# Stick-breaking mixer: the product of each unit's first head moves from VectorE to GpSimd

## The chip, the cores and the metric

The kernel runs on one core of a Trainium2 chip. The metric is the device time of one launch in microseconds (us). Three runs of the kernel before took 3267.1, 3270.11 and 3271.65 us; the median is 3270.11 us. Engines are called by the names of the profile: PE (TensorE), DVE (VectorE), ACT (ScalarE), POOL (GpSimd), SP (SyncE).

## The reference

One inference step of a two-layer encoder, for a prompt of 1024 rows and a sample of 64 rows that has 256 cached rows. The change lies in one of four mixers, the stick-breaking attention with 8 heads of width 64:

```
def sb_core(k, v, k_pos, q, q_pos):
    z = einsum('bqhd,bshd->bhqs', q, k) * HEAD_DIM ** -0.5
    mask = k_pos < q_pos
    log_beta = log_sigmoid(z)
    log_1m = where(mask, log_sigmoid(-z), 0.0)
    after = cumsum(log_1m, axis=3, reverse=True) - log_1m
    a = where(mask, exp(log_beta + after), 0.0)
    return einsum('bhqs,bshd->bqhd', a, v)
```

So a weight is sigmoid(z) of its key, times the product of sigmoid(-z) over all later keys that are still before the query. All is float32.

## The kernel before

The kernel is a row of phases (projections, attentions, feed-forward), and each phase is a block of one instruction stream per engine. The first instruction of a phase stands behind the end of the phase before on all engines. The attention phases come from one function, `attention(kind)`; the change touches kind "d", the stick-breaking one, called `stick` in the code; its tiles are named att_d_... in the trace.

The work of this phase is cut into 36 units: 4 pairs of heads, and in each pair 9 query tiles (`ALL`). Tile t (0 to 7) has 128 queries and 128(t+1) keys, so 128 to 1024 columns; the ninth tile is the sample, 64 queries and 320 keys. A unit holds both heads of its pair. For each unit:

- PE makes the scores of both heads in PSUM (L1059, with the mask added at L1070).
- ACT makes sigmoid(-z) into `rest` (L1196) and sigmoid(z) into `prob` (L1201), for each head.
- DVE runs along the keys backwards with a running product, `rest` into `left` (`scan`, L1285), and multiplies `prob` by `left` shifted by one column, in place (`weigh`, L1295). `remain(i)` puts both scans of a unit first, then both products. So DVE issues: scan head 0, scan head 1, product head 0, product head 1.
- PE transposes `prob` into PSUM (L1098), ACT copies that to SBUF (L1152), PE multiplies it with the values (L1127), and DVE copies the result out of PSUM (`output`, L1301). There is one PSUM bank for these results, so the product of a unit waits for the copy of the unit before it.

The order on each engine is written out by hand. DVE does `output(i - 2)` and then `remain(i + 2)`. PE transposes unit i, makes the scores of unit i + 3, and multiplies unit i - 1 with its values. There are four `prob` buffers per head, two of `rest` and two of `left`. A scan into `left` waits until the product that read the same buffer, two units back, is done (the semaphore `prob_ready` of its head); the transposes of PE wait for the same semaphore. A product waits for its own scan (`scan_done`) and for ACT's sigmoids (`taken_done`).

GpSimd sets one column of each `left` buffer to 1 in this phase (L1026) and has nothing else to do. In the three other attention phases it scales `prob` by a number per row (L1034, one tensor input), between DVE's reciprocal and PE's transposes.

DVE also has a scan with two SBUF inputs in the phase of kind "b", in which GpSimd scales: `select` (L1363 to L1370), five DVE instructions for each of six tiles, late in that phase.

Of the kernel before, what the change touches and what calls it, by code (L numbers as in the profile page):

```python
# [9 lines left out]
ALU = mybir.AluOpType  # L10
# [8 lines left out]
SEQ, DEC, PAST = 1024, 64, 256  # L19
# [18 lines left out]
FROM = 1  # L38


class Phase:
# [12 lines left out]
    def sb(self, name, shape, dt=F32):  # L54
        return self.ctx.enter_context(self.nc.sbuf_tensor(f"{self.name}_{name}", shape, dt))
# [7 lines left out]
    def sem(self, name):  # L63
        s = self.ctx.enter_context(self.nc.semaphore(f"{self.name}_{name}"))
        self.sems.append(s)
        return s
# [43 lines left out]
def key_tile(t):  # L110

    return (P * (t + 1), 0) if t < NT else (PAST + DEC, SEQ)
# [698 lines left out]
def queries(t):  # L811
    return DEC if t == NT else P
# [9 lines left out]
ALL = [(p, t) for p in range(PAIRS) for t in range(TILES)]  # L822
# [9 lines left out]
def chunks(i):  # L832

    w = key_tile(ALL[i][1])[0]
    return [(0, 0, 512), (1, 512, w - 512)] if w > 512 else [(i % 2, 0, w)]


def chunks_until(i):
    return sum(len(chunks(j)) for j in range(i + 1))
# [50 lines left out]
def attention(nc, dram, consts, kind, src, home, fetch=None):  # L890
# [15 lines left out]
    with Phase(nc, f"att_{kind}") as ph:  # L906
# [17 lines left out]
        ring = ahead + 1  # L924
        prob = [[sb(f"prob{s}{h}", [P, SEQ]) for h in range(2)] for s in range(ring)]
        if mla or fox:
            hidden = sb("hidden", [P, SEQ], BF16)
        if stick:
            rest = [[sb(f"rest{s}{h}", [P, SEQ]) for h in range(2)] for s in range(2)]
            left = [[sb(f"left{s}{h}", [P, SEQ + 1]) for h in range(2)] for s in range(2)]  # L930
# [5 lines left out]
        cleared, staged = sem("cleared"), sem("staged")  # L936
# [3 lines left out]
        prob_ready = [sem(f"prob_ready{h}") for h in range(2)]  # L940
# [7 lines left out]
        if stick:  # L948
            rest_done = [sem(f"rest_done{h}") for h in range(2)]
            taken_done = [sem(f"taken_done{h}") for h in range(2)]  # L950
            scan_done = [sem(f"scan_done{h}") for h in range(2)]
# [39 lines left out]
        @block.sync  # L991
        def _(eng):
            def load_w(p):
                eng.dma_start(wkv[p % 2][:], dram["w_b_ukv"][0, :, p * 2 * P:(p + 1) * 2 * P]).then_inc(w_in[p % 2], 16)

            def load_q(p):
                eng.dma_start(q[p % 2][:], dram["qbT"][2 * p:2 * p + 2].rearrange("h d t -> d h t")).then_inc(q_in[p % 2], 16)

            if fetch is not None:
                if fetch.x is not None:  # L1000
                    eng.dma_start(fetch.x[:], dram["x1"][0:P]).then_inc(fetch.x_in, 16)
                fetch.fetch_soon(eng)
            if mla:
                for p in range(2):
                    load_w(p)
                    load_q(p)
            for i, (p, t) in enumerate(ALL):
                if mla and t == 0 and 0 < p < PAIRS - 1:
                    eng.wait_ge(tp_ready, FROM + groups.jobs[p, 8] + 1)
                    load_w(p + 1)  # L1010
                    for h in range(2):
                        eng.wait_ge(s_ready[h], FROM + i)
                    load_q(p + 1)

        @block.gpsimd
        def _(pool):
            g = nc.gpsimd
            if mla or fox:
                g.memset(hidden[:, 0:SEQ - P], 0.0).then_inc(cleared, 1)
                g.tensor_copy(hidden[:, SEQ - P:], mask[:]).then_inc(cleared, 1)  # L1020
            if fox:
                g.memset(src["qT"][:, :, TOK:], 0.0).then_inc(staged, 1)
            if stick:
                for s in range(2):
                    for h in range(2):
                        g.memset(left[s][h][:, SEQ:SEQ + 1], 1.0).then_inc(cleared, 1)  # L1026
                return
            for i, (p, t) in enumerate(ALL):
                n, w = queries(t), key_tile(t)[0]
                for h in range(2):  # L1030
                    pr = prob[i % ring][h][0:n, 0:w]
                    c = 2 * (i % ring) + h
                    pool.wait_ge(rcp_done[h], FROM + i + 1)
                    g.tensor_scalar(pr, pr, rr[0:n, c:c + 1], 1.0, ALU.mult, ALU.mult).then_inc(prob_ready[h], 1)  # L1034
# [219 lines left out]
        def _(dve):  # L1254
# [23 lines left out]
            def scan(i, h):  # L1278
                p, t = ALL[i]
                n, w = queries(t), key_tile(t)[0]  # L1280
                dve.wait_ge(rest_done[h], FROM + chunks_until(i))
                if i >= 2:
                    dve.wait_ge(prob_ready[h], FROM + i - 1)
                r = rest[i % 2][h][0:n, 0:w][:, ::-1]
                v_.tensor_tensor_scan(left[i % 2][h][0:n, SEQ - w:SEQ][:, ::-1], r, r, 1.0, ALU.mult, ALU.bypass).then_inc(scan_done[h], 1)  # L1285

            def weigh(i, h):
                p, t = ALL[i]
                n, w = queries(t), key_tile(t)[0]
                if i == 0:  # L1290
                    dve.wait_ge(cleared, FROM + 4)
                dve.wait_ge(scan_done[h], FROM + i + 1)
                dve.wait_ge(taken_done[h], FROM + chunks_until(i))
                pr = prob[i % ring][h][0:n, 0:w]
                v_.tensor_tensor(pr, pr, left[i % 2][h][0:n, SEQ - w + 1:SEQ + 1], ALU.mult).then_inc(prob_ready[h], 1)  # L1295

            def output(i):
                p, t = ALL[i]
                n = queries(t)
                dve.wait_ge(pv_done, FROM + i + 1)  # L1300
                v_.tensor_copy(home[:, p, t * P:t * P + n], O[:, 0:n]).then_inc(o_out, 1)  # L1301
# [70 lines left out]
            if stick:  # L1372
                def remain(i):
                    for h in range(2):
                        scan(i, h)
                    for h in range(2):
                        weigh(i, h)

                for i in range(ahead - 1):
                    remain(i)  # L1380
                for i in range(n_units):
                    if i >= 2:
                        output(i - 2)
                    if i + ahead - 1 < n_units:
                        remain(i + ahead - 1)
                for i in (n_units - 2, n_units - 1):
                    output(i)
                return
# [964 lines left out]
```

## Time and profile before

| | |
|---|---|
| median of three runs | 3270.11 us |
| the profiled execution's own time | 3271.4 us |
| its span | 3269.6 us |
| PE busy | 2994.6 us (92%) |
| DVE busy | 1742.8 us (53%) |
| ACT busy | 1280.6 us (39%) |
| POOL busy | 169.4 us (5%) |
| mean granted TensorE clock | 0.955 |

All times in the rows are from one profiled execution. A row of the timeline may merge several like instructions that follow each other (x2). DVE instructions are stamped so that the next often starts 0.08 us before the one in front of it ends. The stick-breaking phase runs from about 2176 to 2341 us of the span.

### The profile page before, as it was taken

What the parts mean: (1) busy time and instruction counts of PE and PEld (TensorE: products, weight loads), DVE (VectorE), ACT (ScalarE), POOL (GpSimd) and SP (SyncE); (2) the same over time, 40 slices, a digit from 0 to 9 for tenths busy, and PEclk for the clock granted to TensorE, in tenths of its full rate; (3) what the DMA queues carried; (4) which work ended last, traced back from release to release, by engine and by line L of the source; (5) the groups of instructions that cost most, each with busy time, mean ns of one, the idle gap of its engine ahead of it and who ended that gap; (6) DMA issues with size and microseconds to landing.
All of it is one profiled execution on the core that took longest, in us unless ns stands there. A gap on an engine that the chain in (4) does not pass through costs nothing. (4 is left out here: it accounts for less than half of the span.)

```text
span 3269.6 us, 48973 instructions
## 1 busy us (share of the span) xinstructions
PE 2994.6 (92%) x17421; PEld 2533.1 (77%) x17421; DVE 1742.8 (53%) x3767; ACT 1280.6 (39%) x2682; POOL 169.4 (5%) x240
## 2 busy tenths in 40 slices
PE   6984887799899999999989798988898999999998
PEld 5771445468899999999989566865688999999998
DVE  4438788765455444444441465148754444444545
ACT  4334787463322222222243355357533222222223
POOL 0000222330000000000000131000000000000000
PEclk9995999899999999999989799999999999999999
DMA  4110100101211111111221201120201111111112
GB/s 133 51 33 3 37 13 1 46 30 47 69 51 38 51 38 38 51 38 51 79 96 55 85 2 49 52 71 1 76 0 52 51 38 39 51 38 51 38 38 75
DMA packets 147231, 152.09 MB, mean 47 GB/s; under 512 B 18156, under 2 KB 123236, under 8 KB 147108
## 3 DMA queue, kind: packets, MB, share of 16 engines
q1 hardware_dynamic: 147108, 150.54, 15.0%
q8 instruction: 66, 1.08, 0.1%
q14 instruction: 57, 0.47, 0.0%
HBM read 126.75 MB, written 23.24 MB: 46 GB/s over the span
## 5 line engine op out<-in xcount | busy, mean ns | idle before, releaser
L223 PE MATMUL ffn_up<-hlow_r,ffn_uhi 128*128 128x384 f32 (+1 forms) x2112 | 691.5, 327 | 0.0
L2107 DVE SCALAR_TENSOR_TENSOR ffn_cv<-ffn_G,ffn_ctap,ffn_cv 128x256 f32<-128x256 f32 (+1 forms) x352 | 168.9, 501 | 493.0 <-ACT ffn_cv L2033 488.3
L223 PEld LDWEIGHTS ffn_up<-hlow_r,ffn_uhi 128*128 128x128 f32 x2112 | 398.3, 189 | 0.9
L2027 ACT ACTIVATE ffn_G<-ffn_up 128x384 f32<-128x384 f32 (+2 forms) x176 | 65.3, 398 | 824.0 <-PE ffn_up L224 824.0
L2140 DVE TENSOR_TENSOR xres<-ffn_dn,xres 128x512 f32<-128x512 f32 (+1 forms) x396 | 263.6, 687 | 132.5 <-PE ffn_dn L224 121.2
L222 PE MATMUL ffn_dn<-ffn_dhi,ffn_ahi 128*128 128x512 f32 x704 | 280.7, 399 | 2.9
L224 PE MATMUL ffn_dn<-ffn_dhi,ffn_alo 128*128 128x512 f32 x704 | 278.3, 395 | 0.0
L223 PE MATMUL ffn_dn<-ffn_dlo_r,ffn_ahi 128*128 128x512 f32 x704 | 278.3, 395 | 0.0
L222 PE MATMUL ffn_up<-mixed_c_r,ffn_uhi 128*128 128x384 f32 (+1 forms) x528 | 174.6, 331 | 5.9 <-DVE ulo_r L2084 5.9
L222 PE MATMUL ffn_up<-mixed_a_r,ffn_uhi 128*128 128x384 f32 (+1 forms) x528 | 174.6, 331 | 5.7 <-DVE ulo_r L2084 5.7
L222 PE MATMUL ffn_up<-mixed_b_r,ffn_uhi 128*128 128x384 f32 (+1 forms) x528 | 174.2, 330 | 0.0
L222 PE MATMUL ffn_up<-mixed_d_r,ffn_uhi 128*128 128x384 f32 (+1 forms) x528 | 174.0, 330 | 0.0
L222 PEld LDWEIGHTS ffn_dn<-ffn_dhi,ffn_ahi 128*128 128x128 f32 x704 | 132.2, 188 | 42.4 <-DVE xres L2140 12.5
L224 PEld LDWEIGHTS ffn_dn<-ffn_dhi,ffn_alo 128*128 128x128 f32 x704 | 132.2, 188 | 32.0
L223 PEld LDWEIGHTS ffn_dn<-ffn_dlo_r,ffn_ahi 128*128 128x128 f32 x704 | 132.3, 188 | 29.9
L2038 ACT ACTIVATE ffn_cv<-ffn_cv 128x384 f32<-128x384 f32 x132 | 67.0, 508 | 182.4 <-DVE ffn_cv L2107 182.4
L222 PE MATMUL out_mm<-out_whi,out_ahi 128*128 128x512 f32 x256 | 104.0, 406 | 9.1 <-DVE wo_even_r L1803 4.6
L2119 DVE TENSOR_TENSOR ffn_alo<-ffn_cv,ffn_ahi 128x384 fp32r<-128x384 f32 x132 | 68.0, 515 | 77.5 <-ACT ffn_ahi L2042 77.5
L2114 DVE TENSOR_TENSOR ffn_cv<-ffn_up,ffn_cv 128x384 f32<-128x384 f32 x132 | 70.8, 536 | 69.1 <-ACT ffn_cv L2038 69.1
L2033 ACT ACTIVATE ffn_cv<-ffn_G,ffn_ctap 128x384 f32<-128x384 f32 (+2 forms) x176 | 103.6, 612 | 4.4
L222 PEld LDWEIGHTS ffn_up<-mixed_c_r,ffn_uhi 128*128 128x128 f32 x528 | 99.6, 189 | 6.7 <-DVE ulo_r L2084 6.3
L222 PEld LDWEIGHTS ffn_up<-mixed_a_r,ffn_uhi 128*128 128x128 f32 x528 | 99.6, 189 | 6.6 <-DVE ulo_r L2084 6.1
(474 smaller groups left out, 6965.9 us busy)
## 6 DMA issues: line engine op xcount, KB each, us to landing
ulo<-in_w_up_dram SPq DMA_DIRECT2D x44, 512.0 KB, 5.0
ffn_ulo<-in_w_up_dram SPq DMA_DIRECT2D x44, 512.0 KB, 4.7
ffn_dlo<-in_w_down_dram SPq DMA_DIRECT2D x22, 1024.0 KB, 4.9
w_d<-in_w_in_odd_dram SPq DMA_DIRECT2D x7, 768.0 KB, 9.9
proj_even_x<-in_x_prompt_dram SPq DMA_DIRECT2D x8, 512.0 KB, 3.4
xres<-in_x_prompt_dram SPq DMA_DIRECT2D x8, 512.0 KB, 4.5
scratch_x<-xres SPq DMA_DIRECT2D x8, 512.0 KB, 3.5
x_d<-scratch_x SPq DMA_DIRECT2D x8, 512.0 KB, 3.9
```

Of the source, the lines that this page charges most:

```text
L222: nc.tensor.matmul(out, lh, rh, start=first, stop=False)
L223: nc.tensor.matmul(out, lh, rl, start=False, stop=False)
L224: return nc.tensor.matmul(out, ll, rh, start=False, stop=last)
L2027: s.activation(G[:, g0:g0 + w], upbank(c, b, 0)[:, j:j + w], ACT.Copy).then_inc(g_out, 1)
L2033: last = s.activation(cv[:, 0, j:j + w], G[:, g0 - 2:g0 - 2 + w], ACT.Identity, scale=ctap[:, c, 0:1], bias=ctap[:, c, 3:4])
L2038: s.activation(cv[:, 1, 0:n], cv[:, 0, 0:n], ACT.Silu).then_inc(silu_done, 1)
L2107: last = v.scalar_tensor_tensor(cv[:, 0, j:j + w], G[:, g0 - 2 + tapno:g0 - 2 + tapno + w], ctap[:, c, tapno:tapno + 1], cv[:, 0, j:j + w] ...
L2114: v.tensor_tensor(cv[:, 1, 0:n0], upbank(c, b, 1)[:, 0:n0], cv[:, 1, 0:n0], ALU.mult).then_inc(a_done, 1)
L2119: last = v.tensor_tensor(to, cv[:, 1, c0 - t0:c1 - t0], ahi[:, c, c0:c1].bitcast(F32), ALU.subtract)
L2140: v.tensor_tensor(xs, dn[j % 4][0:n, :], xs, ALU.add).then_inc(half_added if t == NT else dn_added, 1)
```

## The change

GpSimd makes the product of head 0 of every unit; DVE keeps both scans and the product of head 1. The waits, the buffers and the semaphores that are raised are the same; the product of head 0 now raises `prob_ready[0]` from GpSimd.

```
             if stick:
                 ... memset of the column of ones
+                pool.wait_ge(cleared, FROM + 4)
+                for i, (p, t) in enumerate(ALL):
+                    n, w = queries(t), key_tile(t)[0]
+                    pool.wait_ge(scan_done[0], FROM + i + 1)
+                    pool.wait_ge(taken_done[0], FROM + chunks_until(i))
+                    pr = prob[i % ring][0][0:n, 0:w]
+                    g.tensor_tensor(pr, pr, left[i % 2][0][0:n, SEQ - w + 1:SEQ + 1], ALU.mult).then_inc(prob_ready[0], 1)
                 return
...
                 def remain(i):
                     for h in range(2):
                         scan(i, h)
-                    for h in range(2):
-                        weigh(i, h)
+                    weigh(i, 1)
```

## Rows read from the trace of the kernel before

**Rows 1.** Windows: busy us and instruction count of each engine in stretches of the phase
```profile
core 0: us, PE busy (x) PEld busy (x) DVE busy (x) ACT busy (x) POOL busy (x), PEclk, DMA share, GB/s
2177.00:2341.00 164.00, 138.69 (x1213) 91.18 (x1212) 140.05 (x180) 122.98 (x322) 0.00 (x0) 0.95 0.06 24
2218.03:2257.23 39.20, 32.54 (x309) 21.53 (x307) 34.90 (x46) 30.52 (x80) 0.00 (x0) 1.00 0.01 2
2221.35:2250.87 29.52, 23.00 (x186) 13.95 (x184) 29.03 (x31) 24.95 (x64) 0.00 (x0) 1.00 0.00 1
```
**Rows 2.** Waits around the phase: who for whom, us in total, times, longest
```profile
DVE mixed_d L1301 <- PE att_d_o L1127: 21.7, 11, 4.2
PE att_d_o L1127 <- DVE mixed_d L1301: 14.6, 9, 3.7
ACT L1196 <- PEq L74: 3.2, 1, 3.2
ACT out_ahi L1770 <- PEq L74: 3.0, 1, 3.0
```
**Rows 3.** Timeline of DVE alone, from the widest unit to the next pair
```profile
2244.04 4.47 DVE L1285 TENSOR_TENSOR_SCAN att_d_left<-att_d_rest 128x1024 f32<-128x1024 f32 x2
2248.42 2.34 DVE L1295 TENSOR_TENSOR att_d_prob<-att_d_prob,att_d_left 128x1024 f32<-128x1024 f32 x2
2250.67 0.29 DVE L1301 COPY mixed_d<-att_d_o 128x128 f32<-128x128 f32 x1
2250.87 1.52 DVE L1285 TENSOR_TENSOR_SCAN att_d_left<-att_d_rest 64x320 f32<-64x320 f32 x2
2252.32 0.86 DVE L1295 TENSOR_TENSOR att_d_prob<-att_d_prob,att_d_left 64x320 f32<-64x320 f32 x2
2253.31 0.72 DVE L1285 TENSOR_TENSOR_SCAN att_d_left<-att_d_rest 128x128 f32<-128x128 f32 x2
2253.95 0.46 DVE L1295 TENSOR_TENSOR att_d_prob<-att_d_prob,att_d_left 128x128 f32<-128x128 f32 x2
2257.02 0.29 DVE L1301 COPY mixed_d<-att_d_o 128x128 f32<-128x128 f32 x1 [2.61 <-PE att_d_o L1127]
2258.41 0.73 DVE L1295 TENSOR_TENSOR att_d_prob<-att_d_prob,att_d_left 128x256 f32<-128x256 f32 x2
2260.34 0.29 DVE L1301 COPY mixed_d<-att_d_o 128x128 f32<-128x128 f32 x1 [1.20 <-PE att_d_o L1127]
```
**Rows 4.** Windows of L1295 alone: the products of one pair's six wide units
```profile
2221.00:2251.00 30.00, 10.02 (x12) 1.00 0.00 1
```
**Rows 5.** Groups by form: one-input GpSimd instructions: busy us, mean ns, idle before
```profile
L1034 POOL TENSOR_SCALAR att_a_prob<-att_a_prob,att_a_rr 128x1024 f32<-128x1024 f32 x8 | 9.0, 1124 | 12.7 <-DVE att_a_rr L1276 12.7
L1034 POOL TENSOR_SCALAR att_a_prob<-att_a_prob,att_a_rr 128x384 f32<-128x384 f32 x8 | 4.7, 588 | 6.1 <-DVE att_a_rr L1276 6.1
L1034 POOL TENSOR_SCALAR att_a_prob<-att_a_prob,att_a_rr 64x320 f32<-64x320 f32 x8 | 4.2, 528 | 9.7 <-DVE att_a_rr L1276 9.2
L1020 POOL COPY att_b_hidden<-mask_chunk 128x128 bf16<-128x128 bf16 x1 | 0.9, 915 | 0.0
L1020 POOL COPY att_c_hidden<-mask_causal 128x128 bf16<-128x128 bf16 x1 | 0.3, 293 | 0.0
```
**Rows 6.** Timelines of GpSimd and of DVE around 565 us, in phase "b"
```profile
565.20 1.41 POOL L1034 TENSOR_SCALAR att_b_prob<-att_b_prob,att_b_rr 64x320 f32<-64x320 f32 x1 [0.23 <-DVE att_b_rr L1276]
...
565.03 0.66 DVE L1363 TENSOR_SCALAR att_b_tie<-scores,top_bits 128x896 bf16<-128x896 f32 x1
565.61 0.67 DVE L1364 TENSOR_SCALAR att_b_below<-scores,top_bits 128x896 bf16<-128x896 f32 x1
566.21 2.27 DVE L1366 TENSOR_TENSOR_SCAN att_b_beyond<-att_b_tie,att_b_spare 128x896 bf16<-128x896 bf16 x1
568.51 1.09 DVE L1368 SCALAR_TENSOR_TENSOR att_b_beyond<-att_b_beyond,att_b_tie 128x896 bf16<-128x896 bf16 x1
```
**Rows 7.** Groups by form: the same scan at the two neighbouring widths
```profile
L1366 DVE TENSOR_TENSOR_SCAN att_b_beyond<-att_b_tie,att_b_spare 128x1024 bf16<-128x1024 bf16 x1 | 2.3, 2347 | 0.0
L1366 DVE TENSOR_TENSOR_SCAN att_b_beyond<-att_b_tie,att_b_spare 128x768 bf16<-128x768 bf16 x1 | 1.8, 1805 | 0.0
```

## The prediction

> **What bounds the kernel now.** Over the whole span PE is the busy engine, but the change lies in one phase, so I read that phase alone. First the waits at its two ends: ACT's first instruction waits for the release of the phase before, and so does its first in the phase behind [rows 2]. What this phase loses or gains therefore goes into the span in full, with nothing else beside it to hide it. Then the windows: in the phase's 164.00 us DVE is busy for 140.05, PE for 138.69, ACT for 122.98 and GpSimd for nothing [rows 1]. These shares are too near each other to name the bound, so the next window holds one period of a pair of heads (39.20 us, DVE 34.90) and the last one only its six wide units, 384 to 1024 columns: 29.03 of 29.52 us on DVE, against 24.95 on ACT and 23.00 on PE. There DVE is the bound without a gap. The rest of the period is the turn from pair to pair (the units of 320, 128 and 256 columns). There DVE waits for PE before its copies, 2.61 and 1.20 us in this pair [rows 3], 21.7 us in the phase, at most 4.2 us at once [rows 2]. PE in turn waits 14.6 us for those copies [rows 2], because there is one bank for its results and each copy stands in DVE's queue behind a whole unit of scans and products. So the time of a wide unit is DVE's own queue; the time of the turn is a chain through PE, in which a little more work on DVE is free.
>
> **What goes.** DVE loses 36 products, one per unit. The twelve products of a pair's six wide units keep it busy for 10.02 us [rows 4]. A pair of products runs 0.09 us into the copy behind it (2248.42 + 2.34 against 2250.67, [rows 3]), six times, so six products give back (10.02 - 0.52) / 2 = 4.75 us per pair of heads. For the four pairs that is 19.0 us. What the products of the narrow units give back (0.43, 0.23 and 0.36 us, half of the rows of 320, 128 and 256 columns in [rows 3]) falls into DVE's waits for PE, where it gains nothing.
>
> **What comes, on GpSimd.** It has 36 products of two float32 tensors, behind nothing but the four memsets. No row shows such an instruction, so I bound it. One-input instructions take 588 ns at 384 columns and 1124 ns at 1024 [rows 5]: 0.8375 ns per column and 266 ns beside that. Six wide units have 4224 columns. If the second input were free, six products would take 4224 x 0.8375 + 6 x 266 ns = 5.1 us. If the two inputs are read one after the other, only the streaming doubles: 8.7 us. If all of it doubles: 10.3 us. If reads and write take turns, three passes: 12.2 us. I take 9.5 us, between the two forms of doubling, since the second tensor is as large as the first; the ends that I keep are 5.1 and 12.2. A GpSimd product of 1024 columns is then some 2.2 us (between 2.0 and 2.25).
>
> The Trainium skill, "GPSIMD Engine Reference", section "Performance versus the Vector engine", gives 4497 ns for a product-like instruction of two float32 tensors at 2048 columns; as an estimate from that page, six wide units are 4224 x 2.196 ns = 9.3 us, and by it the sum below would be +18 us. No run here shows it yet.
>
> **Does it run beside DVE?** That decides the sign. The trace has one place where a GpSimd instruction meets DVE instructions whose operands all lie in SBUF. At 565.20 us a GpSimd scaling of 64x320, which takes 528 ns elsewhere [rows 5], took 1.41 us [rows 6]. It ended at 566.61, 0.40 us after the second of two DVE instructions had given way to the scan at 566.21; so it stood still for 0.88 us while DVE worked. And the scan that followed took 2.27 us, where the mean of its neighbours at 1024 and 768 columns is (2.347 + 1.805) / 2 = 2.08 us [rows 7]: it lost 0.19 us while GpSimd finished. Each waited for the other. DVE's two instructions ahead of it kept their usual pace (0.66 and 0.67 us). In the changed phase every instruction of DVE but the short copy out of PSUM has two inputs in SBUF, as this scan has. So I take it that GpSimd's product and DVE's scans and products run one after the other.
>
> The Trainium skill's page "SBUF — State Buffer", section "SBUF: two separate sides", goes further than this row: the pair of ports is held for the whole instruction, by a DVE instruction with two SBUF inputs too when GpSimd reads SBUF, and the other side blocks fully. The one meeting agrees with it by 0.88 and 0.19 us; that a float32 scan of 2.3 us holds GpSimd off from end to end is not shown by any row. By that rule alone the change cannot gain from overlap, and it speaks against it.
>
> **The sum.** GpSimd's product of head 0 is released when scan 0 ends. Scan 1 is by then already running (DVE's instructions follow each other without a gap, [rows 3]), so GpSimd stands until scan 1 ends. DVE's next instruction, the product of head 1, now waits for the scan directly in front of it, and such a wait leaves a gap: in [rows 6] the instruction behind the scan starts 0.03 us after its end instead of 0.08 before it. Into this gap GpSimd's waiting product steps, and DVE's product stands behind it; behind that in DVE's queue are the copy of a result, for which PE waits, and the next unit's scans. Whether GpSimd gets in here or one instruction later, a wide unit is two scans, one GpSimd product, one DVE product and a copy, in a row. Per pair: 9.5 - 4.75 = +4.75 us; four pairs: +19.0 us. In the first pair the units of 128 and 256 columns have no turn to hide in: about 0.5 us. In the later turns the three narrow units add about 0.3 us each, under the waits of 2.61 and 1.20 us. The new wait of a scan on `prob_ready` of head 0 is two units old by then, and costs nothing. PE's transposes see head 0 earlier than head 1, as before. A first use on GpSimd may cost something once (the first copy took 915 ns, a later one 293, [rows 5]): 0.6 us, under the 2-unit lead. DMA does nothing in this phase that matters (share 0.06, [rows 1]).
>
> So 3271.4 + 19.5 = 3290.9 us for the profiled execution, whose own time lies 1.3 us above the median of the runs; the forecast for the median is 3270.1 + 19 = 3289 us. By the two bounds of GpSimd's price: 4 x (5.1 - 4.75) = +1.6 and 4 x (12.2 - 4.75) = +30 us.
>
> **The rivals.**
> - *No exclusion for these instructions.* The scan passes one column in 2.2 ns (4.47 us for two of 1024), half the pace of the product, and may leave GpSimd room; then the product of 2.2 us is done while scan 1 (2.2 us) and product 1 still run, and DVE is lighter by 4.75 us per pair, less six gaps of 0.11 us: 4.1. A wide stretch of 29.52 us becomes 25.4, and ACT with its 24.95 us just fits. Four pairs: -16.4 us, 3254 us; if ACT's order costs half of that, 3262. It decides from the point at which GpSimd's product of 1024 columns ends within 3.4 us (scan 1 and product 1) while scan 1 keeps its 2.2 us. For it: the one meeting is short, its scan is bf16, and the two DVE instructions that held GpSimd off had one input, not two. Against it: that scan did lose 0.19 us.
> - *Exclusion, but GpSimd's product is as cheap as DVE's.* At the lower bound, 5.1 against 4.75 us, the exchange is even: +1.6 us, 3272. A mixture, in which GpSimd gets half of its time beside the scan, ends there as well: 4 x (9.5 / 2 - 4.75) = 0. For it: the one-input rows are within a tenth of DVE's product (1124 against some 1170 ns). Against it: two inputs are twice the reading.
> - *Exclusion with dearer turns.* At the upper bound, 3301 us.
>
> **How the numbers follow.** The forecast, serial running at 8.7 to 12.2 us per pair, has 0.73; its own range is 3281 to 3301. Even exchange or half overlap: 0.12. No exclusion: 0.15. About 0.2%, 6.5 us, is what a measurement of this kernel can tell from no change. Faster by more than that holds most of the last case, 0.14; within it lie the even exchange and the weak end of the last case, 0.13; slower 0.73. The range reaches from 3258, the middle of the no-exclusion case, to 3303, the upper bound with one first-use cost.
>
> **What would show it.** Right: in the wide units the gap between scan 1 and DVE's product of head 1, or the length of that product, is about 2 us at 1024 columns; GpSimd's instructions are stamped longer than 2.2 us, since they wait from the end of scan 0; the stretch of six wide units is some 34 us and DVE's waits for PE in the turns get shorter. Wrong: DVE's product starts 0.03 us after scan 1 and takes its 1.2 us while GpSimd's runs beside it, and the stretch shrinks towards 25 us. The prediction fails on its price if the exclusion is seen but GpSimd's product costs far from 2.2 us at 1024 columns, and on its place if the turns, not the wide units, grow.

## The result, and the profile after

Twenty runs of the changed kernel have a median of 3274.3 us, twenty of the kernel before 3268.84 us: the ratio is 1.0016, 95% interval 1.0010 to 1.0022, so 3 to 7 us more. The forecast was 3289 us in a range of 3258 to 3303: the sign is right, the size is not, 5.5 us against 19.

Four windows of the changed kernel, cut as before at the start of the scans of 320 and of 384 columns: a turn from one pair of heads to the next, the next pair's six wide units (a wide stretch), the turn behind it, and the end of the phase. The first number is the length, then come the busy us by engine; PEclk is the granted clock as a share of full.

```profile
core 0: us, PE busy (x) PEld busy (x) DVE busy (x) ACT busy (x) POOL busy (x), PEclk, DMA share, GB/s
2207.70:2218.94 11.24, 11.10 (x120) 8.77 (x120) 5.91 (x13) 5.67 (x16) 2.56 (x3) 0.85 0.01 1
2218.94:2250.40 31.46, 24.53 (x186) 15.34 (x184) 31.16 (x26) 24.85 (x64) 15.97 (x6) 0.95 0.00 1
2250.40:2260.07 9.67, 9.54 (x120) 7.58 (x120) 5.91 (x14) 5.57 (x16) 2.57 (x3) 1.00 0.01 2
2332.49:2344.30 11.81, 11.02 (x118) 9.80 (x118) 3.47 (x8) 4.32 (x9) 1.18 (x1) 0.75 0.01 1
```

Two turns of the kernel before:

```profile
2210.12:2221.35 11.23, 11.09 (x120) 8.51 (x120) 5.87 (x16) 5.68 (x16) 0.00 (x0) 0.85 0.01 2
2250.87:2260.55 9.68, 9.54 (x120) 7.58 (x120) 5.88 (x17) 5.57 (x16) 0.00 (x0) 1.00 0.01 2
```

The wide stretch that took 29.52 us [rows 1] takes 31.46, and DVE is busy for all but 0.30 us of it. All four: 28.93, 29.52, 28.93 and 29.52 before, 31.40, 31.46, 31.29 and 31.46 after, 116.90 against 125.61, +8.71 us or 2.18 per pair. The turn is a chain through PE as before (9.67 and 11.24 us; before 9.68 and 11.23): GpSimd's 2.56 us of work in it do not show. What differs between turns is the granted clock, 1.00 or 0.85.

DVE and GpSimd in the widest unit of that stretch, from the timelines of each engine alone:

```profile
2242.94 4.46 DVE L1292 TENSOR_TENSOR_SCAN att_d_left<-att_d_rest 128x1024 f32<-128x1024 f32 x2
2247.43 2.84 DVE L1302 TENSOR_TENSOR att_d_prob<-att_d_prob,att_d_left 128x1024 f32<-128x1024 f32 x1
2250.20 0.28 DVE L1308 COPY mixed_d<-att_d_o 128x128 f32<-128x128 f32 x1
...
2245.29 3.90 POOL L1033 TENSOR_TENSOR att_d_prob<-att_d_prob,att_d_left 128x1024 f32<-128x1024 f32 x1 [3.42 <-DVE att_d_left L1292]
```

These rows answer to the first three of [rows 3]. The two scans keep their pace (4.46 us, 4.47 before). GpSimd's product (in brackets its idle time before, and what ended it) is issued at 2245.29, while scan 1 runs, and ends at 2249.19, 1.79 us after the scan's end at 2247.40. DVE's product starts at 2247.43 and takes 2.84 us where one took 1.21: it stood for 1.63 us, and it ends 1.08 us behind GpSimd's. In all this is the order that was forecast, scan, scan, GpSimd's product, DVE's product, copy. The groups by form give the same at both ends of the widths (the mean ns of one instruction is the number before the last bar; L1295 is DVE's product in the kernel before):

```profile
L1033 POOL TENSOR_TENSOR att_d_prob<-att_d_prob,att_d_left 128x1024 f32<-128x1024 f32 x4 | 15.6, 3898 | 13.7 <-DVE att_d_left L1292 13.7
L1302 DVE TENSOR_TENSOR att_d_prob<-att_d_prob,att_d_left 128x1024 f32<-128x1024 f32 x4 | 11.4, 2842 | 0.1
L1033 POOL TENSOR_TENSOR att_d_prob<-att_d_prob,att_d_left 128x384 f32<-128x384 f32 x4 | 5.7, 1427 | 9.3 <-DVE att_d_left L1292 9.3
L1302 DVE TENSOR_TENSOR att_d_prob<-att_d_prob,att_d_left 128x384 f32<-128x384 f32 x4 | 4.2, 1040 | 0.1
L1295 DVE TENSOR_TENSOR att_d_prob<-att_d_prob,att_d_left 128x1024 f32<-128x1024 f32 x8 | 9.3, 1210 | 0.0
L1295 DVE TENSOR_TENSOR att_d_prob<-att_d_prob,att_d_left 128x384 f32<-128x384 f32 x8 | 4.0, 543 | 0.0
```

DVE's product is held 1.63 us at 1024 columns (2842 ns against 1210 before) and 0.50 at 384 (1040 against 543): 1.77 ns per column less 0.18 us. Over the six widths the held time is 11.65 - 5.26 = 6.4 us per pair (the sums of the means after and before), where the forecast has 9.5.

### The profile page after: what moved, and what is told of

Read it like the earlier page. It is cut to its first block and busy times, and to the rows that moved or that the text cites. A ratio compares the mean times of both kernels' runs of the same rounds, so it can differ in the third digit from the quotient of the medians.

```text
span 3273.4 us, 48973 instructions
## 1 busy us (share of the span) xinstructions
PE 2996.9 (92%) x17421; PEld 2535.6 (77%) x17421; DVE 1751.1 (53%) x3731; ACT 1280.4 (39%) x2682; POOL 242.8 (7%) x276
## 3 DMA queue, kind: packets, MB, share of 16 engines
q8 instruction: 66, 1.08, 0.1%
```

## Experiments

Two explanations are tried first. Theory A: GpSimd and DVE exclude each other in full, and only GpSimd's price was set too high. Theory B: the price was right, and a part of GpSimd's product runs beside DVE's scan.

**GpSimd's product alone.** Four more products at the end of the changed kernel's phase:

```
+                pool.wait_ge(prob_ready[1], FROM + n_units)
+                for j, w in enumerate((1024, 768, 512, 384)):
+                    g.tensor_tensor(rest[j // 2][j % 2][:, 0:w], left[0][0][:, 0:w], left[1][1][:, 0:w], ALU.mult)
```

> The changed kernel, and behind its last product GpSimd makes four more products of two float32 tensors (1024, 768, 512, 384 columns) into buffers that are no longer used, while DVE only copies results out of PSUM; they change no output. Theory A (full exclusion, GpSimd's price was set too high): alone, 1024 columns take about 1.8 us, which is the time from the end of DVE's second scan to the end of GpSimd's product in the changed kernel (2247.40 to 2249.19), with 1.7 to 1.8 ns per column between the widths. Theory B (the price of 2.2 us was right, and part of the product runs beside the scan): alone, 1024 columns take 2.2 us or more.

Groups by form of this run:

```profile
L1036 POOL TENSOR_TENSOR att_d_rest<-att_d_left 128x1024 f32<-128x1024 f32 x1 | 2.4, 2351 | 0.4 <-DVE att_d_prob L1305 0.4
L1036 POOL TENSOR_TENSOR att_d_rest<-att_d_left 128x384 f32<-128x384 f32 x1 | 1.0, 996 | 0.0
```

It spoke for theory B: 2.35 us alone, 2.117 ns per column. But these products had other operands than the kernel's, so a later run took the forms apart.

**The same operands as in the kernel, alone.** Five products at the end of the phase:

```
+                pool.wait_ge(prob_ready[1], FROM + n_units)
+                pool.wait_ge(tp_ready, FROM + groups.transposed(n_units - 1))
+                for w in (1024, 384):
+                    g.tensor_tensor(rest[w // 1024][0][:, 0:w], prob[2][0][:, 0:w], left[0][0][:, SEQ - w + 1:SEQ + 1], ALU.mult)
+                for w in (1024, 384):
+                    pr = prob[1 + w // 1024][1][:, 0:w]
+                    g.tensor_tensor(pr, pr, left[0][0][:, SEQ - w + 1:SEQ + 1], ALU.mult)
+                g.tensor_tensor(rest[0][1][:], left[0][0][:, 0:SEQ], left[1][1][:, 0:SEQ], ALU.mult)
```

> The changed kernel, and behind its last unit GpSimd makes five more products while DVE only copies results out of PSUM; they change no output: prob times shifted left into another buffer (1024 and 384 columns), the same in place (1024 and 384 columns), and left times left unshifted into another buffer (1024, as in the first run alone, 2.35 us). Question: why GpSimd, 2.35 us alone, needs only 1.79 us behind the end of scan 1. Theory C (the form sets the rate): in place and shifted takes some 1.95 us at 1024 and 0.83 at 384 columns, 1.77 ns per column, and the unshifted form 2.35 again. Theory D (the form is not it; a part of the product is done while DVE runs): all forms take 2.35 and 1.00 us.

```profile
L1041 POOL TENSOR_TENSOR att_d_rest<-att_d_left 128x1024 f32<-128x1024 f32 x1 | 2.3, 2337 | 0.0
L1037 POOL TENSOR_TENSOR att_d_rest<-att_d_prob,att_d_left 128x1024 f32<-128x1024 f32 x1 | 2.0, 1999 | 3.9 <-PE att_d_tp L1113 3.9
L1040 POOL TENSOR_TENSOR att_d_prob<-att_d_prob,att_d_left 128x1024 f32<-128x1024 f32 x1 | 2.0, 1998 | 0.0
L1040 POOL TENSOR_TENSOR att_d_prob<-att_d_prob,att_d_left 128x384 f32<-128x384 f32 x1 | 0.9, 864 | 0.0
```

Theory C holds: the kernel's form takes 2.00 and 0.86 us, 1.772 ns per column and 0.18 us beside, in place or not; the unshifted product of two `left` buffers takes 2.34 again. So the hold grows with the width as the instruction does (1.77 ns per column in both), and only a fixed part of the instruction does not hold DVE: the hold is 0.37 us shorter at 1024 columns (2.00 - 1.63) and at 384 (0.864 - 0.497). Nothing that grows with the width runs beside the scan, and theory B falls. Why the unshifted form streams slower was not pursued.

**One input in place of two** (head 0 is scaled by the column of ones and so left unweighted):

```
-                    g.tensor_tensor(pr, pr, left[i % 2][0][0:n, SEQ - w + 1:SEQ + 1], ALU.mult).then_inc(prob_ready[0], 1)
+                    g.tensor_scalar(pr, pr, left[i % 2][0][0:n, SEQ:SEQ + 1], 1.0, ALU.mult, ALU.mult).then_inc(prob_ready[0], 1)
```

> The changed kernel, but GpSimd scales head 0 by the column of ones (one tensor input) in place of the product, so head 0 is left unweighted. Theory A: GpSimd holds DVE off for as long as it reads, so half of what the product cost: DVE's product of 1024 columns takes about 2.0 us (2.84 in the changed kernel, 1.21 before), the six wide units of a pair take about 28.3 us (31.4 with the product, 29.5 before), and the run is some 12 us below the changed kernel, near 3262. Theory B: the one-input instruction (1.12 us alone) is done beside the scan of 2.2 us, DVE's product is back at 1.2 us, the six wide units take about 25.5 us, the run is near 3252.

```profile
L1302 DVE TENSOR_TENSOR att_d_prob<-att_d_prob,att_d_left 128x1024 f32<-128x1024 f32 x4 | 7.8, 1959 | 0.1
L1302 DVE TENSOR_TENSOR att_d_prob<-att_d_prob,att_d_left 128x384 f32<-128x384 f32 x4 | 3.0, 760 | 0.1
```

DVE's product takes 1.96 us, as theory A has it: held 0.75 us at 1024 and 0.22 at 384, 0.83 ns per column, the one-input streaming of [rows 5] (0.8375). The wide stretches took 27.80, 28.65, 27.83 and 28.65 us. They came out as expected, but the time was missed: 3267.9 us instead of 3262, ratio to the kernel before 0.9991 (0.9981 to 1.0001). In the profiled run (3268.4 us) two turns took 12.37 us, at a granted clock of 0.76.

**The heads exchanged** (GpSimd makes head 1's product, DVE head 0's):

```
-                    pool.wait_ge(scan_done[0], FROM + i + 1)
+                    pool.wait_ge(scan_done[1], FROM + i + 1)
...
-                    weigh(i, 1)
+                    weigh(i, 0)
```

> The changed kernel with the heads exchanged: GpSimd makes the product of head 1 and DVE that of head 0, which does not wait for the scan just in front of it. Theory A: DVE's product starts 0.08 us before the end of scan 1 and takes 1.21 us at 1024 columns; GpSimd's waits for it, is stamped some 2.8 us long, and now holds off the next unit's first scan by 1.6 us less the copy out of PSUM of 0.2 us, which needs no second port and runs beside it. Per wide unit this saves the gap of 0.11 us and up to 0.2 us: six wide units take about 29.7 us (31.4 in the changed kernel), the run is about 7 us below the changed kernel, near 3268 and the same as before. Theory B: the next scan is not held off in full, and the stretch is shorter than before, under 28 us.

Timelines of this run, DVE and then GpSimd:

```profile
2237.36 5.84 DVE L1292 TENSOR_TENSOR_SCAN att_d_left<-att_d_rest 128x1024 f32<-128x1024 f32 x2
2243.12 1.19 DVE L1302 TENSOR_TENSOR att_d_prob<-att_d_prob,att_d_left 128x1024 f32<-128x1024 f32 x1
2244.24 0.28 DVE L1308 COPY mixed_d<-att_d_o 128x128 f32<-128x128 f32 x1
2244.44 3.13 DVE L1292 TENSOR_TENSOR_SCAN att_d_left<-att_d_rest 64x320 f32<-64x320 f32 x2
...
2243.28 2.89 POOL L1033 TENSOR_TENSOR att_d_prob<-att_d_prob,att_d_left 128x1024 f32<-128x1024 f32 x1 [4.41 <-DVE att_d_left L1292]
```

As theory A has it: DVE's product is back at 1.19 us; the copy out of PSUM keeps its 0.28 us while GpSimd reads; the next two scans of 320 columns take 3.13 us instead of 1.52, held 1.61. The wide stretches took 28.82 and 29.25 us, a little under the kernel before; the run has the ratio 0.9994 (0.9985 to 1.0003), no difference that can be measured. The stretch is shorter than the 29.7 us expected: the hold of each pair's widest unit, 1.6 us, now falls on the scans of 320 columns, in the turn, where it is hidden (a turn at full granted clock took 9.67 us here too).

**What is removed, without what comes instead** (GpSimd's product covers one column, the rest of head 0 is left unweighted):

```
-                    g.tensor_tensor(pr, pr, left[i % 2][0][0:n, SEQ - w + 1:SEQ + 1], ALU.mult).then_inc(prob_ready[0], 1)
+                    g.tensor_tensor(pr[:, 0:1], pr[:, 0:1], left[i % 2][0][0:n, SEQ - w + 1:SEQ - w + 2], ALU.mult).then_inc(prob_ready[0], 1)
```

> The changed kernel, but GpSimd's product covers one column only, so the rest of head 0 is left unweighted: what is removed from DVE without what comes instead. Forecast's own terms: six wide units give back 4.75 us less six gaps of 0.11, 29.5 to 25.4 us, and ACT with 24.95 us of work just fits; the run is some 16 us below the kernel before, near 3252. If instead ACT or PE takes over as the bound, the stretch stays above 27 us and the run at 3258 or more.

```profile
2211.16:2237.52 26.36, 22.93 (x186) 13.96 (x184) 24.96 (x26) 24.10 (x63) 8.52 (x6) 1.00 0.00 1
2237.52:2247.20 9.68, 9.54 (x120) 7.58 (x120) 5.26 (x14) 6.32 (x18) 1.33 (x3) 1.00 0.01 2
```

3248.8 us, ratio 0.994 (0.9926 to 0.9954): about 20 us less. The wide stretches gave 12.35 us in all, not the 16.4 of the rival without exclusion: DVE is busy for 24.96 of 26.36 us, and waits 1.12 us for ACT's sigmoids (ACT is busy for 24.1) ahead of the scans of 640 columns. Of the rest 4.8 us came from the turns, all at full granted clock here: 38.1 us with the phase's end, against 42.9 before.

The widest unit of this stretch, DVE and then GpSimd, shows the other side of the exclusion:

```profile
2231.68 4.46 DVE L1292 TENSOR_TENSOR_SCAN att_d_left<-att_d_rest 128x1024 f32<-128x1024 f32 x2
2236.17 1.23 DVE L1302 TENSOR_TENSOR att_d_prob<-att_d_prob,att_d_left 128x1024 f32<-128x1024 f32 x1
...
2234.03 2.09 POOL L1033 TENSOR_TENSOR att_d_prob<-att_d_prob,att_d_left 128x1 f32<-128x1 f32 x1 [3.62 <-DVE att_d_left L1292]
```

A product of a single column, issued while scan 1 runs, takes 2.09 us: it ends at 2236.12, where the scan ends (2236.14). So the scan keeps GpSimd off for its whole length, and the little that GpSimd then has to do does not hold DVE's product (1.23 us).

**Both kernels once more, unchanged.**

> The kernel before, unchanged, for a second profile: the wide stretches 28.9 and 29.5 us again (fixed by DVE), the turns 9.7 at full granted clock and 11.2 to 12.4 below it; the phase starts within 5 us of 2175, which would say that the 4.9 us by which the changed kernel's profile enters the phase earlier are the clock of earlier phases and not the change.

> The changed kernel, unchanged, for a second profile and a second comparison: the four wide stretches 125.6 us in all, 8.7 above the kernel before; the run 3 to 8 us above it, the difference to 8.7 lying in the turns and in other phases with the granted clock.

A wide stretch and the turn behind it, of the kernel before and then of the changed kernel:

```profile
2216.87:2246.40 29.53, 23.01 (x186) 13.97 (x184) 29.03 (x32) 24.95 (x64) 0.00 (x0) 1.00 0.00 1
2246.40:2257.61 11.21, 11.08 (x120) 8.97 (x120) 5.95 (x16) 5.57 (x16) 0.00 (x0) 0.85 0.01 1
```
```profile
2219.10:2250.56 31.46, 25.78 (x186) 16.30 (x184) 31.16 (x25) 25.12 (x64) 15.99 (x6) 0.89 0.00 1
2250.56:2260.22 9.66, 9.53 (x120) 7.58 (x120) 5.91 (x13) 5.57 (x16) 2.57 (x3) 1.00 0.01 2
```

The wide stretches repeat: 117.46 us in all before (one of them 0.5 us longer than in the first profile) and 125.47 after. The turns with the phase's end do not: 42.86 and 43.72 us before; 42.39 after, 42.39 and 38.08 in the two runs with products added at the end, 38.06 here. The second comparison gave 1.0010 (1.0001 to 1.0019). The kernel before entered this phase at 2172.99 us, beside 2177.79 in its first profile and 2171.8 to 2174.8 in all the others, so the 4.9 us by which the changed kernel's profile is early there belongs to the one profile of before.

**An earlier copy.** The kernel before with DVE's copy of a result between the scans and the products:

```
                     for h in range(2):
                         scan(i, h)
+                    if i >= ahead:
+                        output(i - ahead)
                     for h in range(2):
                         weigh(i, h)
...
                 for i in range(n_units):
-                    if i >= 2:
-                        output(i - 2)
                     if i + ahead - 1 < n_units:
                         remain(i + ahead - 1)
-                for i in (n_units - 2, n_units - 1):
+                for i in range(n_units - ahead, n_units):
                     output(i)
```

> The kernel before, with only DVE's copy of a result moved forward by two products: scan, scan, copy, product, product. PE waits 14.6 us in all for these copies in the turns from pair to pair. Theory E (the turn is a chain through the copy): PE multiplies the values while DVE still makes the last wide unit's products, each turn gets some 2 us shorter (11.2 to about 9, and 9.7 to about 8), the wide stretches stay at 28.9 to 29.5 us, and the run gains about 6 to 8 us: 3262. Rival: the copy now waits for PE inside a unit, the wide stretches grow by as much, and the run is at 3269 or above.

```profile
2216.47:2245.40 28.93, 24.37 (x212) 15.34 (x208) 28.93 (x32) 24.51 (x62) 0.00 (x0) 1.00 0.00 1
2245.40:2253.90 8.50, 8.28 (x96) 6.16 (x96) 5.91 (x16) 6.13 (x18) 0.00 (x0) 1.00 0.01 2
```

And from the waits of the phase (in total, times, longest):

```profile
PE att_d_o L1127 <- DVE mixed_d L1301: 8.0, 5, 2.5
```

3257.2 us, ratio 0.9968 (0.9955 to 0.9980): this beats both kernels. The turns take 8.50 us, PE waits 8.0 us for copies instead of 14.6 [rows 2], and the wide stretches stay at 28.93 (one at 29.84). The turns with the phase's end are 32.8 us in all against 42.9. In this profile they ran at full granted clock as well, and the two can be told apart: at full clock turns and end of the old order take 38.1 us (in the run with one column and in the changed kernel's second profile), so the order gives 5.3 us and the clock the other 4.8.

**The change on top of the earlier copy**, beside the earlier copy alone:

> The change made on the kernel with the early copy: DVE does scan, scan, copy, product of head 1; GpSimd the product of head 0. In the kernel with the early copy the granted clock stayed at full level through every turn, so the change's own cost can be read without the clock. Theory A: GpSimd reads beside the copy out of PSUM (0.18 us, not slowed), then holds DVE's product; per pair 6.4 us held plus 0.66 of gaps, less 1.1 of copies and 4.75 of removed products = +1.2 us: wide stretches 30.1 us against 28.93, the run 5 us above the early copy without the change, near 3262. If the copy does not run beside GpSimd, +2.2 us per pair and 3266. Rival (the change costs nothing where the clock does not fall): 3257.

> The early copy without the change once more, beside the run above on the same chip: 3257 us, wide stretches of 28.93 us, turns of 8.50 us at full granted clock.

A wide stretch of the first, then a wide stretch and a turn of the second:

```profile
2252.82:2282.98 30.16, 25.64 (x210) 15.69 (x209) 30.16 (x25) 24.35 (x63) 15.98 (x6) 0.97 0.01 1
```
```profile
2253.36:2282.29 28.93, 24.84 (x204) 15.57 (x202) 28.93 (x31) 24.19 (x62) 0.00 (x0) 0.95 0.01 2
2282.29:2293.12 10.83, 10.83 (x108) 7.87 (x104) 5.90 (x16) 6.13 (x18) 0.00 (x0) 0.82 0.01 2
```

The wide stretches agree with theory A: 121.00 against 115.75 us, +1.31 per pair where +1.2 was expected, so the copy does run beside GpSimd. The medians are 3261.6 us (0.9983, 0.9974 to 0.9992) and 3260.3 us (0.9971, 0.9962 to 0.9980): 1.3 us apart, the means 3.2 us, where 5 were expected. The intervals overlap, so the runs do not settle what the change costs here. In these two profiles the turns with the end go the other way, 32.5 us with the change and 36.3 without. That the earlier copy always keeps the clock at full level in its turns was wrong: here one took 9.69 and one 10.83 us, at 0.93 and 0.82.

## Why the prediction was right or wrong

*What bounds the phase* was right: the wide stretches are DVE's queue, before and after, and the narrow units' work disappears in the turns (11.24 and 9.67 us as before).

*Exclusion* was right, and is shown from both sides. DVE's product is held for 1.63 us; with one input the hold is about half (0.75), and with the heads exchanged it moves to the next scan (1.61). In turn scan 1 holds even a product of one column until its end. The place was right too: GpSimd gets in at the gap behind scan 1. The Trainium skill's "SBUF — State Buffer" ("SBUF: two separate sides") says that whichever starts first has the shared pair of ports for its whole instruction. For float32 scans the runs agree (GpSimd's product ends 1.79 us after scan 1), with one difference: DVE is not held for the whole GpSimd instruction but for 0.37 us less.

*The step that failed* is "I take 9.5 us, between the two forms of doubling", the price of GpSimd's six products per pair, which the sum then puts into DVE's queue in full. Both were too much. The price: alone and in the kernel's form the six products take 4224 x 1.772 ns + 6 x 0.18 us = 8.6 us, 0.9 less and close to the first form of doubling (8.7). The overlap: DVE is held for only 6.4 of these 8.6 us, 2.2 less, because a fixed 0.37 us of each product lies outside the hold; the prediction let the 266 ns that it found beside the streaming, or twice that, hold DVE like the streaming. The sum with the measured terms, per pair: 6.4 held, 0.66 for six gaps of 0.11 us (which the prediction put under the hold, but which come on top of it), less 4.75: +2.3. Measured are +2.18; two of the stretches before had a wait for ACT of 0.5 us, which took up some. Four pairs give +8.7 us instead of +19. The lower bound that the prediction kept (5.1 us) was nearer to the 6.4 than its 9.5. The Trainium skill's "GPSIMD Engine Reference" ("Performance versus the Vector engine") gives 4497 ns for 2048 columns; an estimate from that, 2.25 us at 1024, lies near the run for one choice of operands (2.351 us), not for the kernel's (2.00).

Two sums of the prediction do not come out as written: 8.7 us per pair gives 3270.1 + 15.8 = 3286 us, not the 3281 at which its serial case begins, and 12.2 us gives 3300, not 3301. Nothing else hangs on them.

*The first pair's 0.5 us* was wrong: its narrow units took 3.40 us before and after.

*From 8.7 to 5.5 us.* The wide stretches cost 8.0 to 8.7 us more in every profile, but the medians of the runs differ by 5.5 us and, the second time, by 3.7. The turns may account for it: with the end of the phase they took 43.3 us on average over two profiles before and 40.2 over four with the change's wide stretches, 3.1 us less, at work that is the same to 0.02 us where the granted clock is 1.00. But two of these four took 42.39 us and two 38.1, so the average is hardly surer than the difference. From the first wide stretch on, the phase took 159.8 and 161.2 us before and 168.0, 168.0, 163.6 and 163.5 after, on average 5.3 us more. In one profile of the changed kernel the low clock fell into the wide stretches (0.84 to 0.89 in all four), where DVE sets the time and it costs nothing. This was not in the prediction. That it is the cause of the difference is inferred from six profiles and not shown; why the low clock falls where it does stays open.

*No exclusion* is out by the holds. The rival's own price was too good as well: with next to nothing left for GpSimd to do, waits for ACT leave 12.35 of the 16.4 us. *Even exchange* is out as a mechanism: six products take 8.6 us alone, not 5.1, and a quarter of that, not half, runs beside DVE. Its 3272 us came nearer to the measured 3274.3 than the forecast did, but in part by luck: by the wide stretches alone the time would be 3270.1 + 8.7 = 3278.8.

## What to carry to other kernels

Where VectorE's instructions have two SBUF inputs, as here, work moved to GpSimd is not taken off VectorE's queue: count GpSimd's streaming time as VectorE's own and compare it with the product that it replaces (1.77 against 1.04 ns per column here). A part that does not grow with the width need not hold VectorE (0.37 us of each product here). Measure an operation alone with the operands of the kernel. And where a queue has a short copy that another engine waits for, its place in the queue can be worth more than the work in it: here the medians fell by 8 to 12 us in two comparisons, for the same instructions, of which about 5 us can be put down to the order itself.

## What was not expected of the hardware

- The same 120 PE instructions of a turn take 9.67 us at a granted clock of 1.00, 11.0 to 11.3 at 0.85 or 0.86 and 12.37 at 0.76 (a mix of the two levels, 1.2 and 2.4 GHz), while a wide stretch takes 31.46 us at 0.95 and at 0.89. PE had waited for DVE in the wide stretch ahead of a fall (busy for 23.01 of 29.53 us); but in another profile of the same kernel a stretch with 23.00 of 29.52 us [rows 1] was followed by a turn at 1.00.
- GpSimd's product of two `left` buffers from column 0 takes 2.34 us at 1024 columns, that of `prob` and of `left` shifted by one column 2.00.
